# Both layers' memory rows split into high and low parts in the prologue, the second layer's set kept in DRAM and loaded whole

## The reference, cut to what matters

```python
for l in range(DEPTH):                                    # DEPTH = 2
    mem_n = rms_norm(mem_prompt, norm_mem[l])             # (1, 256, 1024)
    mk = (mem_n @ w_mem_k[l]).reshape(bp, N_MEM, H_X, HD_X)
    mv = (mem_n @ w_mem_v[l]).reshape(bp, N_MEM, H_X, HD_X)
    hp, ... = decoder_layer(hp, pos_prompt, mk, mv, ...)
    # in it: h = h + 0.5 * ffn1(h); m = token_mixing(h, mk, mv, ...)
    #        merged = sum_i sigmoid(gate_i) * (o_i @ w_branch_i); m = merged @ w_out
    #        h = h + rms_norm(m); h = h + 0.5 * ffn2(h)
```

## Time and profile before

| | |
|---|---|
| time, median of 3 runs (lowest to highest) | 2172.58 us (2168.78 to 2180.76) |
| the profiled execution's own time | 2193.62 us |
| its span, first to last instruction | 2192.0 us |
| mean granted TensorE clock in it | 0.951 |
| PE matmul busy | 2044.9 us, 93% |
| PE weight loads busy | 1993.3 us, 91% |
| DVE busy | 1340.8 us, 61% |
| ACT busy | 892.4 us, 41% |
| POOL busy | 111.2 us, 5% |
| DMA | 370.92 MB, 42.8% of the engines' time on SP's queue (q1), 12.3% on POOL's (q0) |
| chain that ended last, by engine | PE 71%, DVE 16%, issue 7%, ACT 3%, DMA 1% |

### The profile page before, as it was taken

How to read it: one execution, slowest core, us unless ns; L and a number is a source line. 1 busy time by engine, 2 the same in 40 slices (tenths; PEclk the granted TensorE clock), 3 DMA queues, 4 the chain that set the end, 5 groups by cost and what they waited for, 6 DMA issues and landing times.

```text
span 2192.0 us, 42454 instructions
## 1 busy us (share of the span) xinstructions
PE 2044.9 (93%) x15686; PEld 1993.3 (91%) x15686; DVE 1340.8 (61%) x2001; ACT 892.4 (41%) x961; POOL 111.2 (5%) x173
## 2 busy tenths in 40 slices
PE   4999999899998999899989999999999889989997
PEld 4999998899997998899979999889999889989997
DVE  3665566745547667756566556575454768676655
ACT  2544435223552343544344434341255332544433
POOL 1000000001110100000000000010111000000000
PEclk8999999888999999999999999996899989999998
DMA  6665656545652456566546655573556335536654
GB/s 208 179 186 163 183 171 186 184 137 164 206 183 93 136 186 206 159 175 179 172 150 192 174 172 166 161 246 113 183 166 214 116 116 164 192 123 170 187 158 150
DMA packets 437536, 370.92 MB, mean 169 GB/s; under 512 B 9426, under 2 KB 415316, under 8 KB 437010
## 3 DMA queue, kind: packets, MB, share of 16 engines
q1 hardware_dynamic: 413520, 280.86, 42.8%
q0 software_dynamic: 23856, 87.98, 12.3%
HBM read 343.16 MB, written 25.64 MB: 168 GB/s over the span
## 4 chain that ended last, share of the span: by engine, by line
PE 71%; DVE 16%; issue 7%; ACT 3%; DMA 1%; DVEq 1%; SPq 0%; ACTq 0%
PE proj L600 44%; PE proj L623 4%; PE proj L618 4%; PE proj L619 4%; PE aux L788 3%; PE proj L598 2%; DVE wl L1554 1%; PE aux L650 1%; DVE y L1693 1%; DVE junk L1761 1%; DVE c_t L1998 1%; DVE t_t L2094 1%; PE aux L887 1%; PE aux L721 1%; ACT wh L1156 1%
## 5 line engine op out<-in xcount | busy, mean ns | idle before, releaser
L1554 DVE TENSOR_TENSOR wl<-raw,wh 128x2048 fp32r<-128x2048 f32 (+1 forms) x284 | 608.2, 2142 | 196.8 <-ACT wh L1156 169.7
L1156 ACT CAST wh<-raw 128x2048 fp32r<-128x2048 f32 (+1 forms) x284 | 507.4, 1787 | 475.3 <-PE proj L600 303.9
L600 PE MATMUL proj<-xh,wh 128*128 128x264 f32 x2688 | 421.0, 296 | 4.8 <-ACTq L1248 4.8
L600 PE MATMUL proj<-xl,wh 128*128 128x264 f32 x2688 | 417.5, 293 | 1.9 <-DVEq L1666 1.9
L600 PE MATMUL proj<-xh,wl 128*128 128x264 f32 x2688 | 405.5, 291 | 3.6 <-DVE wl L1554 3.5
L600 PEld LDWEIGHTS proj<-xh,wh 128*128 128x128 f32 x2688 | 364.3, 194 | 14.2 <-issue 6.8
L600 PEld LDWEIGHTS proj<-xl,wh 128*128 128x128 f32 x2688 | 366.0, 194 | 3.2 <-DVEq L1666 3.2
L600 PEld LDWEIGHTS proj<-xh,wl 128*128 128x128 f32 x2688 | 360.7, 193 | 5.3 <-DVE wl L1554 5.3
L619 PE MATMUL proj<-hl,wh 128*128 128x264 f32 x704 | 174.5, 284 | 0.0
L618 PE MATMUL proj<-hh,wh 128*128 128x264 f32 x704 | 174.4, 285 | 0.0
L619 PEld LDWEIGHTS proj<-hl,wh 128*128 128x128 f32 x704 | 132.7, 189 | 0.0
(11 more groups left out here) (388 smaller groups left out, 2595.6 us busy)
## 6 DMA issues: line engine op xcount, KB each, us to landing
raw<-ffn_w_in SPq DMA_DIRECT2D x176, 512.0 KB, 4.9
raw<-w_in SPq DMA_DIRECT2D x80, 1024.0 KB, 5.8
raw<-ffn_w_out SPq DMA_DIRECT2D x64, 704.0 KB, 4.6
sring<-cache_mem_k POOLq DMA_DIRECT2D x32, 512.0 KB, 4.7
sring<-cache_mem_v POOLq DMA_DIRECT2D x32, 512.0 KB, 3.9
out<-sring POOLq DMA_DIRECT2D x32, 512.0 KB, 3.7
sring<-state_gdn POOLq DMA_DIRECT2D x32, 512.0 KB, 5.1
raw<-w_mem_v SPq DMA_DIRECT2D x12, 1024.0 KB, 5.4
```

Source lines behind the costliest of these rows:

```text
L600: mm = pe.matmul(o, w[:, s, k * 256 + t * P:k * 256 + (t + 1) * P], a[:, k, :], **go)
L1156: act.copy(wh[:, slot, 0:size], raw[:, slot, 0:size]).then_inc(hi_done[slot], 1)
L1554: dve.tensor_sub(wl[:, slot, 0:size], raw[:, slot, 0:size], wh[:, slot, 0:size].bitcast(F32)).then_inc(split_done[slot], 1)
```

## The change

The scaling by the gain and the split into high and low parts are done for both layers in the prologue, from `y`, which holds the normalised rows there. Layer 0's parts stay in `memh` and `meml`; layer 1's are made in `saveh` and `savel`, which lie where the feed-forward arrays come later, and POOL stores them into DRAM (`next_h`, `next_l`, 1 MB each). In each pass POOL then loads both straight into `memh` and `meml`, 2 MB, where 1 MB was loaded into `mnt`. These two arrays overlap operands of `b1`, so the loads wait for a new semaphore, `b1_done`, that ACT gives behind group 0 of `out`. ACT's eight and DVE's eight instructions of each pass are gone, and so are the copies of the gain (`gmem`). DVE waits for the stores in front of `f1i`, which overwrites their source. PE waits for the loads in front of `mva`. Each tile's products with the high weights come before that with the low weights, which is so in the kernel before too: no row of PE moves.

```diff
--- before.py
+++ after.py
@@ -111,7 +111,7 @@
 MILESTONES = ("sq rt sqp rtp mem_split x1 xn1 x2 xn2 x3 xn3 "
               "mvn mkt_all mkn1 ab_in ab_neg ab_exp gb_done mqt mmx mpe msr mpr mpT mqs moh ksth vsth sall smx stz rprod gprod gu gkst rgs "
               "spe spr sptd glr_prompt gates_in gsqt conv_p "
-              "x_half sq_half y_half y_all xh_half xh_all memhi o_mem merged rraw rot rvt rkd rvn rvsd rp rS_out rof rsq rlr o_ret "
+              "x_half sq_half y_half y_all xh_half xh_all memhi b1_done o_mem merged rraw rot rvt rkd rvn rvsd rp rS_out rof rsq rlr o_ret "
               "conv_s gsq gqr gqk tail cso bcd gexp geb dm dme g_at "
               "gvb gvnd gvn0d gsg gvb1 gvn1d gqd gS_out gof g2sq glr o_gdn ").split()
 
@@ -121,7 +121,7 @@
           ffn_in, ffn_out, tables, outs):
     (y_prompt, y_sample, ret_p, gdn_p, conv_p, mk_p, mv_p, ret_s, gdn_s, conv_s) = outs
     (t_ident, t_swap, t_tri, t_masks, t_rot, t_dec, t_kdec, t_sel) = tables
-    mem_t = nc.dram_tensor("mem_t", (P, KT, NM), F32).ap()
+    next_h, next_l = (nc.dram_tensor(n, (P, KT, NM), F32R).ap() for n in ("next_h", "next_l"))
     ctx = ExitStack()
     with ctx:
         def sb(name, shape, dt=F32):
@@ -150,7 +150,7 @@
         acc, rt = sb("acc", [P, T]), sb("rt", [P, T])
         full = sb("full", [P, 2, SEQ + 3])
         csum = sb("csum", [P, 16, NS])
-        gains, gl, gmem = sb("gains", [P, KT, 14]), sb("gl", [P, KT, 7]), sb("gmem", [P, KT, 1])
+        gains, gl = sb("gains", [P, KT, 14]), sb("gl", [P, KT, 7])
         convw, cwl = sb("convw", [P, 16, 2 * CW]), sb("cwl", [P, 16, CW])
         gng, gnl = sb("gng", [P, 2, L]), sb("gnl", [P, 2])
         alog, dtb, epst = sb("alog", [P, L, H]), sb("dtb", [P, L, H]), sb("epst", [P, 1])
@@ -188,7 +188,7 @@
         mvn = at("mvn", 62976, [P, 2, D])
         mkt = at("mkt", 25088, [P, KT, NM])
         sqw = at("sqw", 29184, [P, KT, T])
-        mnt = at("mnt", 16896, [P, KT, NM])
+        saveh, savel = at("saveh", 0, [P, KT, NM], F32R), at("savel", 8192, [P, KT, NM], F32R)
         xnat = at("xnat", 0, [P, 3, D])
         yout = at("yout", 0, [P, 3, D])
         mnat = at("mnat", 12288, [P, 2, D])
@@ -442,8 +442,9 @@
             start_at_one(pool, unit_used)
             pool.memset(kst[:].bitcast(F32), 0.0).then_inc(M["stz"], 1)
             pool.memset(vst[:].bitcast(F32), 0.0).then_inc(M["stz"], 1)
-            pool.wait_ge(pro_dve, 16)
-            pool.dma_start(mem_t, y[:, :, 0:NM]).then_inc(mem_saved, 16)
+            pool.wait_ge(M["mem_split"], 2)
+            pool.dma_start(next_h, saveh[:]).then_inc(mem_saved, 16)
+            pool.dma_start(next_l, savel[:]).then_inc(mem_saved, 16)
 
             def unit(l, n):
                 s, k = n % SRING, n // SRING
@@ -518,10 +519,11 @@
                         unit(l, E_UNIT + b + SRING)
                 store_prompt_state(l, "gS_out", gdn_p, gdn_stored)
 
-                pool.wait_ge(mem_saved, 16)
-                pool.wait_ge(M["o_gdn"], l + 1)
+                pool.wait_ge(mem_saved, 32)
+                pool.wait_ge(M["b1_done"], l + 1)
                 passed(pool)
-                pool.dma_start(mnt[:], mem_t).then_inc(mem_loaded, 16)
+                pool.dma_start(memh[:], next_h).then_inc(mem_loaded, 16)
+                pool.dma_start(meml[:], next_l).then_inc(mem_loaded, 16)
 
                 for s, n in ((mk_stored, 1), (mv_stored, 1), (ret_stored, 1), (gdn_stored, 1), (conv_stored, 2), (state_stored, 2 * NS)):
                     pool.wait_ge(s, (l + 1) * (16 * n))
@@ -1094,7 +1096,7 @@
                         pe.wait_ge(M["merged"], l * KT + k + 1)
                 products(l, "out", mh, ml, early=merged_tiles)
                 total(l, "p2", "sqp")
-                pe.wait_ge(M["mem_split"], l + 2)
+                pe.wait_ge(mem_loaded, 32 * (l + 1))
                 products(l, "mva", memh, meml, "natural", groups=(0,))
                 square_total(l, 3)
                 products(l, "mva", memh, meml, "natural", groups=(1,))
@@ -1224,17 +1226,18 @@
                         act.sem_inc(sq_ready, 1)
                 return tile
 
-            def scale_memory(layer, src):
+            def scale_memory(layer, out):
 
                 for k in range(KT):
-                    order.apart(act.activation(memh[:, k, :], src[:, k, 0:NM], ACT.Copy, scale=gains[:, k, bass.ds(layer + 12, 1)]))
+                    order.apart(act.activation(out[:, k, :], y[:, k, 0:NM], ACT.Copy, scale=gains[:, k, layer + 12:layer + 13]))
                 order.wait()
                 act.sem_inc(M["memhi"], 1)
 
             act.wait_ge(pro_dve, 19)
             for s in range(2):
                 split(0, s, 0, GW)
-            scale_memory(0, y)
+            scale_memory(0, memh)
+            scale_memory(1, saveh)
             order.fresh()
             stream(0, "mv0", copied(0, lambda g, t: mvn[:, t, g * 256:(g + 1) * 256]))
             with act.Fori(0, L) as l:
@@ -1494,11 +1497,7 @@
                 stream(l, "g1", copied(l, lambda g, t: g1s[:, 2 * g + t, :], ACT.Sigmoid))
                 tell("gates_in")
                 stream(l, "b1")
-                def next_memory(g):
-                    if g == 0:
-                        act.wait_ge(mem_loaded, 16 * (l + 1))
-                        scale_memory((l + 1) % L, mnt)
-                stream(l, "out", squares(l), after=next_memory, hold=True)
+                stream(l, "out", squares(l), after=lambda g: tell("b1_done") if g == 0 else None, hold=True)
                 order.fresh()
                 result_root(2, "out")
                 squares_around(3, "mva", values(0))
@@ -1544,7 +1543,6 @@
             dve.wait_ge(pro_pe, 19)
             order(cp(gng[:], proj[2][:, 0:4].rearrange("p (j n) -> p j n", n=2)))
             dve.sem_inc(pro_dve, 1)
-            order(cp(gmem[:], gains[:, :, 12:13]))
             dve.sem_inc(M["x_half"], 1)
             dve.sem_inc(M["x1"], 1)
 
@@ -1638,22 +1636,20 @@
                             mid(4 * i + u)
                 return tile
 
-            def split_memory(n, src, tiles=range(KT)):
-
-                if 0 in tiles:
-                    dve.wait_ge(M["memhi"], n)
-                for k in tiles:
-                    order.apart(stt(meml[:, k, :], src[:, k, 0:NM], gmem[:, k, :], memh[:, k, :].bitcast(F32), ALU.mult, ALU.subtract))
+            def split_memory(layer, high, low):
+
+                dve.wait_ge(M["memhi"], layer + 1)
+                for k in range(KT):
+                    order.apart(stt(low[:, k, :], y[:, k, 0:NM], gains[:, k, layer + 12:layer + 13], high[:, k, :].bitcast(F32), ALU.mult, ALU.subtract))
                 order.wait()
-                if KT - 1 in tiles:
-                    dve.sem_inc(M["mem_split"], 1)
+                dve.sem_inc(M["mem_split"], 1)
 
             order.fresh()
             for s in range(2):
                 split(0, s, 0, GW)
-            split_memory(1, y)
+            split_memory(0, memh, meml)
+            split_memory(1, saveh, savel)
             stream(0, "mv0")
-            dve.wait_ge(mem_saved, 16)
             dve.wait_ge(M["stz"], 2)
             with dve.Fori(0, L) as l:
                 def ready(name):
@@ -1721,6 +1717,7 @@
 
                 norm_x(1, 0, lambda: stream(l, "mvb", groups=(0,)))
                 stream(l, "mvb", groups=(1,))
+                dve.wait_ge(mem_saved, 32)
                 stream(l, "f1i", hidden_tile(l, True))
                 order(dve.memset(acc[:], 0.0))
                 stream(l, "f1o", result_tile(l, 1, "sqp"), hold=True)
@@ -2189,9 +2186,7 @@
                         tell("merged")
                 stream(l, "b1", merge_delta)
                 order(dve.memset(acc[:], 0.0))
-                order(cp(gmem[:], gains[:, :, bass.ds((l + 1) % L + 12, 1)]))
-                stream(l, "out", result_tile(l, 3, "sqp"), hold=True,
-                       late=lambda g: split_memory(l + 2, mnt, range(4 * g, 4 * g + 4)) if g < 2 else None)
+                stream(l, "out", result_tile(l, 3, "sqp"), hold=True)
                 add_result(2, "x3")
                 held_split(l, "out")
                 norm_x(3, 4, lambda: stream(l, "mva", groups=(0,)))
```

## The result

Median 2151.22 us (2149.22 to 2156.94, 6 runs) against 2173.97 us (2168.78 to 2180.76, 6 runs) of the kernel before: a ratio of 0.9884, 95% interval 0.9859 to 0.9909. That is 22.75 us faster where I had forecast 6.6. Ten further runs of the changed kernel gave 2153.17 us, ratio 0.9930 (0.9898 to 0.9962).

The account below looks back on a forecast made before the run. PE, busy 93%, was taken as the bound, waiting on DVE in `b1` and `out`. Gains of 5.9 us there and 2.0 for the clock, less 1.3 in the prologue, made 6.6 us faster: 2166 us, range 2156 to 2178.

Parts of the forecast that it names:

- What bounds the kernel: PE, busy 93% of the span; in the edited stretch it waits for DVE early in `out` and before p2.
- Load out of `b1`: In `b1`, the late weight load falls to 5.2 us, gaining 1.6 us in layer 0 and 1.4 in layer 1.
- Sixteen out of `out`: End of `out`: removing ACT's and DVE's instructions gains at most 2.7 us a layer, limited by the `w_mem_v` load's landing.
- my worst: In `out`, the upper bound for the `w_mem_v` load's landing: 13.3 us.
- the 11 us that I had named as a sign of being wrong: In `out`, the forecast counted as wrong if the `w_mem_v` load took over 11 us.
- Clock behind `b1`: Products behind the waits in `b1`: less half clock on PE, 2.0 us gained, bounds 0 and 4.9.
- Prologue: Stores and queued loads delay the first `ffn_w_in` load: 1.3 us lost, 5.8 if it takes 13.3 us.
- the 13.3 us of the earlier trace: Prologue's load against 4 MB from POOL; at that time the first `ffn_w_in` load would cost 5.8 us.
- The step that failed: Prologue: eight more instructions each on ACT and DVE, covered by idle times of 8.56 and 10.45 us; `gmem` copies cost nothing.
- That PE's order of products would move the time is no rival: no PE row changes place: Over the kernel: a changed order of PE's products was ruled out as a rival, with no size or chance given.
- The rivals: Whole kernel: all gains arrive, 2159 us (0.26); no change, 2172 (0.10); moved transfers starve weight loads, 2182 (0.10).
- The range: Whole time: 2156 to 2178 us, taking in the all-gains rival, most of no change, and some spread of runs.

Follow-up runs that it names:

- e11: e9 with a third 1 MB transfer, its data unused, issued where the old load was: 2152.96 us, ratio 0.9896.
- e1: The kernel before, unchanged, profiled in another execution: 2172.63 us, ratio 1.0001.
- e10: The kernel before with 74 matmuls a layer, results unread, put where PE waits for DVE in `gq`: 2156.51 us, ratio 0.9923.
- e17: The kernel before with DVE's first memset done seven times more in idle time at 1 us: 2161.27 us, ratio 0.9957.
- e3: The changed kernel with the unused buffer `gmem` allocated again where it stood: 2155.03 us, ratio 0.9914.
- e9: The changed kernel with 74 matmuls a layer, results unread, put where PE waits for DVE in `gq`: 2149.62 us, ratio 0.9881.
- e16: The changed kernel measured once more, in ten runs: 2153.17 us, ratio 0.9930.
- e18: The changed kernel with DVE's first memset done twice more in idle time at 1 us: 2169.63 us, ratio 0.9981.
- e12: e9 with each layer's first four state units and the two tables (3 MB) asked for only after `x2`: 2174.46 us, ratio 0.9984.
- e4: The changed kernel with eight ACT and eight DVE instructions of the old forms back in `out`: 2173.81 us, ratio 0.9987.
- e2: The kernel before with two DVE reciprocals added in the prologue ahead of the first square root: 2175.12 us, ratio 1.0002.

## Why the prediction was wrong, step by step

- **What bounds the kernel.** Right for `b1` and `out`, but I read only there. I saw the profile's lower clock, put it down to that one execution, and never asked where in the span it was low.
- **Load out of `b1`: right.** Landing in 5.2 us was forecast, 5.64 and 5.22 came; e11 puts the load back and gets `b1` 1.7 to 2.8 us longer.
- **Sixteen out of `out`: right.** The wait for p2 fell to 2.54 and 1.85 us, against 1.9 to 3.7 forecast. `w_mem_v` landed 8 us behind its issue (860.89 to 868.84), where I took 9. The second `w_mem_v` load took 14.21 us, more than my worst and more than the 11 us that I had named as a sign of being wrong, but `mva` took only 0.4 us longer.
- **Clock behind `b1`: too small if anything.** I took 5.9 + 2.0 = 7.9 us for all of `b1` and `out`. The mean of `b1` with `out` is 55.2 and 53.3 us in four profiles of the kernel before (the first, e1, e10, e17) and 50.3 and 48.7 in five of the changed one (the first, e3, e9, e16, e18): 4.9 + 4.6 = 9.5 us.
- **Prologue: right in kind, wrong in size.** Taken 1.3 us, bound 5.8; in the same profiles `f1i` begins at 70.7 and 73.9 us, so it lost 3.2 us. The cast waits 3.81 us on `ffn_w_in` as the 13.3 us of the earlier trace rows had warned; I chose near the lower end without a row for it. e12, with 3 MB of the loads on POOL's queue asked for later, begins `f1i` at 71.1 us where it was 75.3 in e9, so these loads are the cause.
- **The sum of these is 9.5 - 3.2 = 6.3 us, against 6.6.** That it comes so near is in part luck: 1.6 us too little in `b1` and `out` and 1.9 too little lost in the prologue cancel. e9 and e10 give 6.9; the changed kernel (e16) against e17, both without the pause, 2161.27 - 2153.17 = 8.1, or 5.9 by the ratios, since they stand in different sets.
- **The step that failed** is the cost of DVE's eight added instructions and the `gmem` copy: "They stand in front of idle times ... which cover them" and "The `gmem` copies lie in idle time: nothing." Their time is covered. What they did was to move every later DVE instruction by seven places, which took a pause of 0.36 us out of `gq`'s chain and with it, in most executions, the slow form of `gq` and `x2`. e17 gets 9.6 us (2 to 17) by that alone. Between my 6.6 and the measured 20.6 to 22.8 (e3, e16 and the first result) lie 14 to 16 us; e17 shows 9.6 of them, and the rest is within the scatter of the runs and not shown by itself. "That PE's order of products would move the time is no rival: no PE row changes place" was true, and the same sentence about DVE would have been false.
- **The rivals.** None held. The range ended at 2156, 5 us too high, since it had no term for anything outside the edited stretch.

## What to carry to other kernels

Before costing an edit, look where the granted clock is low over the whole span and which wait stands ahead of each such stretch: here a pause of 0.36 us ahead of the wait for `sptd`, taken out of the chain, went with 9.6 us a run (e17). Take a second profile of the unchanged kernel: here the first had the slow form in both layers (200.4 us each), and the next, e1, took 192.6 and 183.2. And when a result is larger than its parts, shift the instruction stream by a few free instructions in both kernels before believing any story: here it moved the time by 10 us one way and by 11 to 16 the other.

## What the runs showed of the hardware

DVE stands still for about 0.36 us more than otherwise at places that keep their number in its instruction stream: 0.59 us idle ahead of `qkvt` in the kernel before against 0.22 in the changed one, 0.62 ahead of `rot` in e18 against 0.25. In the changed kernel, where number 825 comes behind 0.71 us of `rot`, nothing is seen of it (0.04 us idle); in e4 and e18 it comes behind 0.71 us of `sqt` and is whole (0.45), so the length of the instruction ahead does not decide alone whether it shows. Another such pause of the kernel before stands ahead of the first score of `rqk`, where DVE is idle for 0.78 us and in the changed kernel for 0.39. The places keep an even spacing: those seen in layer 0 between `rqk` and `out`, in kernels whose streams are shifted against each other, stand ahead of numbers 569, 825, 953, 1081, 1337, 1465, 1593, 1721 and 1849 of DVE's instructions, all a multiple of 128 apart. DVE is idle there for 0.40 to 0.47 us (0.26 at 825 in e2), where the same row of a kernel with another shift shows 0.04 to 0.09. The packets inside the span on queue q14 have 8 KB each (0.53 MB in 65), those on q8, the other queue called instruction, 16 KB (1.56 MB in 95).

The same kernel's runs spread over up to 34 us (2156.17 to 2190.24 in one set of 31). The profiles show where: `gq` with `x2` takes between 182.8 and 200.4 us a layer with equal work, 17.6 us in each of two layers.

Filling PE's waits kept the clock at 0.98 to 0.99 over `gq` and `x2` in e9 and gained nothing over the fast form (182 to 183.5 us against 182.8 to 184.5). It did not take away the slow one: four of the eight layers profiled in e9 to e12 still took 196 us, where the slow form takes up to 200.4. The quickest version tried was e9 at 2149.62 us (4 runs), which cannot be told from the changed kernel.
